# The last expert's rows kept in the second half, and the two halves added to the residual apart

## The chip, the core and the metric

The program runs on one core of a Trainium2 chip. The metric is the device time of one execution in microseconds; it covers two trunk layers for 128 context tokens and 256 latent tokens, that is three tiles of 128 tokens.

## What is computed

```python
def trunk_layer(x, cond, p, mixer, rope, ctx):
    sh1, sc1, g1, sh2, sc2, g2 = adaln(cond, p['w_ada'], p['b_ada'])
    h = rms_norm(x, p['g_norm1']) * (1 + sc1) + sh1
    y, state = mixer(h, p, rope, ctx)
    x = x + g1 * y
    h = rms_norm(x, p['g_norm2']) * (1 + sc2) + sh2
    x = x + g2 * hier_moe(h, p)          # the change is here
    return x, state

def hier_moe(h, p):                      # 4 groups of 8 experts, best group, best 2 experts in it
    ...
    wk, ik = lax.top_k(pe, TOP_K)
    wk = wk / jnp.sum(wk, -1, keepdims=True)
    ...
    hh = jax.nn.silu(h1) * h3 * gate[:, :, None].astype(t.dtype)
    return jnp.einsum('tef,efd->td', hh, p['w2']).reshape(bn, n, d)
```

Layer 0's mixer is a gated MLP beside windowed attention, layer 1's is latent attention: projections of the normed tiles to 672 latent columns, their expansion to heads, attention. All is float32. Each token goes through two of 32 experts; the product with a gate may be done after the expert.

## The kernel before

All orders are written out by hand. Each engine has its own program, and they wait for one another's semaphores. SyncE issues nearly all loads in a fixed order: an order that waits holds up all loads behind it. GpSimd issues the gathers and the stores of expert rows.

**Experts.** Experts are taken in 32 steps; step e computes expert e // 2 + e % 2 * 16, so the last step is that of expert 31. Each has 64 token places; what doesn't fit goes to overflow blocks. Per step: TensorE multiplies 64 tokens by w1 and w3 (L943, 32 records), ScalarE and VectorE form silu(h1) * h3 (L1604, L2350), TensorE transposes it (L949) and multiplies by w2 (L956), ScalarE copies the result to one of two buffers (L1618), and GpSimd stores it row by row to `expert_rows` in HBM (L2826). This tensor has two halves of 384 rows: a token's first pick is written to row t of the first half and its second pick to the same row of the second half. `row_numbers`, worked out in VectorE's `router` for all tokens and experts, says which. "Expert 30's store" below is that of step 30, "expert 29's" that of step 29. The semaphores `y_out0` and `y_out1` count the stores of even and of odd steps.

**The end of a layer.** SyncE's `rows_stored` (L627) waits until all stores of both buffers have landed. `load_pair` (L633) then loads, for tile t, 128 rows of each half, 512 KB each. `load_state` (L621) loads the residual, which was put into HBM in the meantime, back to `x_tiles`. ScalarE's `scale_pair` (L1669) multiplies the first half by its gate. VectorE's `combine` does three operations of 128 x 1024: adds the gated second half (L2459), multiplies by G, which holds the modulation row g2 (L2462), and adds to the residual (L2464).

**What follows in layer 0.** Layer 1 starts in the same place. TensorE: transposes and two expansions of the cached latents (`transpose_c`, `expand`, L1308), products that nobody reads (`keep_running(8, 2)`, L790), and then per tile the transposes of the normed tile (`transpose_h`, L766) and the projection (`project1`, L1258). Tile 1's transposes stand after twelve of tile 0's sixteen products, tile 2's after twelve of tile 1's. VectorE: evacuation of the latents, `unit(0)` (L2628 to L2641: sums over heads, scales of the keys, with a square root on ScalarE between), `combine(0, 0)`, norm of tile 0 (L1976, L1978, after ScalarE's sum of squares L1508), evacuation with modulation (L2038), `combine(0, 1)`, norm, `unit(1)`, evacuation, `combine(0, 2)`, and so on. ScalarE has its own list with `unit`, `scale_pair`, `rms` and its half of the evacuations.

**At the end of layer 1** nothing follows but the three tiles' `combine` and the stores of the output, which ScalarE issues tile by tile.

## Time and profile before

| | |
|---|---|
| median of 3 runs | 978.43 us (975.48 to 981.66) |
| profiled execution | 978.13 us, span 976.3 us, mean granted clock 0.976 |
| TensorE busy | 896.2 us (92%) |
| VectorE, ScalarE, GpSimd busy | 409.5, 239.9, 120.2 us |
| DMA | 318.85 MB, mean 327 GB/s |

The time of the profiled execution includes 1.83 us around its span (first to last instruction). Busy shares are means over stages with different limits. In rows of the timeline the first number is the start in us, the second the time from the start of the first instruction to the end of the last of the row; in brackets stands how long the engine had been idle and what ended that.

### The profile page before, as it was taken

To read this page: it belongs to the slowest core of one execution; us is meant where nothing else is said; L and a number is where in the kernel's file an instruction comes from. 1 tells how busy PE (TensorE), PEld (TensorE's weight loads), DVE (VectorE), ACT (ScalarE), POOL (GpSimd) and SP (SyncE) were. 2 spreads that over 40 slices of the span, in tenths; PEclk is the share of its full clock that TensorE was granted. 3 is DMA by queue.
4 is the path that set the end of the run, shared out by engine and by line. 5 is a ranking of instruction groups with operands and counts; after the bars stand their busy time and mean duration, and the time that the engine had idled before them with its cause. 6 is when DMAs were issued, how large, how long until landed. Compare 5 with 4: busy or idle time off the path is not lost.

```text
span 976.3 us, 14476 instructions
## 1 busy us (share of the span) xinstructions
PE 896.2 (92%) x5479; PEld 503.0 (52%) x5479; DVE 409.5 (42%) x1193; ACT 239.9 (25%) x605; POOL 120.2 (12%) x131
## 2 busy tenths in 40 slices
PE   6999989999999999888999988999989999998880
PEld 3346447556555565455366554554655555645540
DVE  2112476346522442211364576662764225222114
ACT  4020243112111111111354455442211111111111
POOL 1000000100222221211100000001002222212110
PEclk9999999999999999999999999998999999999996
DMA  9999799739999999998870039507599999999975
GB/s 373 397 406 417 292 419 419 247 142 370 364 416 418 402 417 416 418 419 328 330 254 7 1 116 351 234 1 237 212 419 415 417 418 409 417 417 418 412 297 202
DMA packets 62133, 318.85 MB, mean 327 GB/s; under 512 B 12662, under 2 KB 14198, under 8 KB 32104
## 3 DMA queue, kind: packets, MB, share of 16 engines
q1 hardware_dynamic: 46864, 287.51, 72.7%
q0 software_dynamic: 13328, 25.02, 7.4%
q10 hardware_dynamic: 1872, 5.39, 1.5%
q8 instruction: 45, 0.74, 0.3%
q14 instruction: 24, 0.20, 0.1%
HBM read 312.72 MB, written 26.49 MB: 347 GB/s over the span
## 4 chain that ended last, share of the span: by engine, by line
PE 66%; DMA 19%; DVE 9%; issue 2%; ACT 2%; SPq 1%; ACTq 0%; DVEq 0%; POOLq 0%
PE psum L943 15%; DMA ring<-in_l_w 15%; PE psum L956 9%; PE psum L1185 6%; PE psum L1308 3%; PE psum L892 3%; PE psum L879 3%; PE psum L1317 2%; PE psum L923 2%; DMA ring<-in_l_w_ada 2%; PE psum L790 2%; PE psum L1436 2%; PE psum L726 2%; PE psum L1349 2%; PE psum L1411 1%
## 5 line engine op out<-in xcount | busy, mean ns | idle before, releaser
L943 PE MATMUL psum<-ring,scratch 128*64 128x256 f32 x1744 | 210.5, 393 | 22.1 <-DMA ring<-in_l_w 21.1
L943 PEld LDWEIGHTS psum<-ring,scratch 128*64 128x64 f32 x1744 | 135.8, 141 | 81.4 <-issue 32.0
L2350 DVE TENSOR_TENSOR scratch<-scratch,psum 64x256 f32<-64x256 f32 x64 | 27.1, 424 | 286.1 <-ACT scratch L1604 278.9
L956 PE MATMUL psum<-ring,scratch 128*64 128x512 f32 x464 | 112.1, 603 | 1.9 <-ACT scratch L1652 1.0
L2826 POOL DMA_INDIRECT expert_rows<-scratch,slot_rows x64 | 63.5, 992 | 337.5 <-ACT scratch L1618 332.9
L1604 ACT ACTIVATE scratch<-psum 64x256 f32<-64x256 f32 x64 | 24.0, 375 | 255.9 <-PE psum L943 255.9
L1618 ACT COPY scratch<-psum 128x512 f32<-128x512 f32 x64 | 37.5, 585 | 132.1 <-PE psum L956 129.9
L1185 PE MATMUL psum<-ring,scratch 128*128 128x512 f32 (+1 forms) x168 | 63.6, 533 | 0.0
L956 PEld LDWEIGHTS psum<-ring,scratch 128*64 128x64 f32 x464 | 29.3, 136 | 41.5 <-issue 37.3
L1185 PEld LDWEIGHTS psum<-ring,scratch 128*128 128x128 f32 x168 | 31.1, 191 | 29.7 <-issue 28.7
L2332 DVE COPY scratch<-psum 128x512 f32<-128x512 f32 x64 | 41.4, 687 | 7.8 <-PE psum L905 6.9
L949 PEld LDWEIGHTS psum<-constants,scratch 128*128 128x128 f32 x132 | 13.3, 141 | 53.9 <-issue 44.6
L790 PE MATMUL psum<-constants 128*128 128x512 f32 x64 | 31.9, 635 | 7.8 <-DMA constants<-in_shape_constants 7.2
L1826 ACT ACTIVATE scratch<-psum,softmax_stats,latent_stats 128x384 f32<-128x384 f32 (+1 forms) x48 | 28.3, 595 | 41.9 <-DVE softmax_stats L2679 41.9
L2818 POOL DMA_INDIRECT scale_shift<-token_rows_hbm,slot_tokens x30 | 31.2, 1041 | 51.7 <-DVE slot_tokens L2345 44.4
L923 PE MATMUL psum<-constants,scale_shift 128*128 128x128 f32 x240 | 32.8, 280 | 2.2 <-DMA scale_shift<-token_rows_hbm,slot_tokens 2.2
L923 PEld LDWEIGHTS psum<-constants,scale_shift 128*128 128x128 f32 x240 | 25.7, 141 | 13.8 <-issue 10.8
L726 PE MATMUL psum<-ring,scT 128*32 128x512 f32 x256 | 30.2, 597 | 2.0 <-DMA ring<-in_l_w_ada 2.0
L949 PE MATMUL psum<-constants,scratch 128*128 128x128 f32 x132 | 28.9, 301 | 3.1 <-DVE scratch L2350 3.1
L1258 PE MATMUL psum<-ring,scratch 128*128 128x384 f32 (+1 forms) x96 | 28.1, 448 | 1.7 <-ACT scratch L1538 1.6
L1308 PE MATMUL psum<-ring 128*128 128x512 f32 x64 | 28.7, 594 | 0.6 <-issue 0.6
L879 PE MATMUL psum<-ring,scratch 128*128 128x512 f32 x64 | 27.8, 593 | 0.0
(393 smaller groups left out, 1242.3 us busy)
## 6 DMA issues: line engine op xcount, KB each, us to landing
ring<-in_l_w SPq DMA_DIRECT2D x108, 1024.0 KB
ring<-in_l_w_rows SPq DMA_DIRECT2D x56, 1024.0 KB
ring<-in_l_w_ada SPq DMA_DIRECT2D x39, 1024.0 KB, 4.9
ring<-in_ada_first SPq DMA_DIRECT2D x8, 1024.0 KB
ring<-in_l_w_o SPq DMA_DIRECT2D x8, 1024.0 KB
ring<-in_l_w_in SPq DMA_DIRECT2D x4, 1024.0 KB
gate_rows<-gate_rows_hbm POOLq DMA_DIRECT2D x8, 512.0 KB, 7.6
scale_shift<-gate_rows_hbm POOLq DMA_DIRECT2D x8, 512.0 KB, 9.9
```

The lines of the kernel that those rows point to most:

```text
L726: last = nc.tensor.matmul(ps[32 * j:32 * j + 32, ada_bank(l, r), :], scT[:, k, :], ring[:, unit % RING, j * 512:(j + 1) * 512], start=k == ...
L790: nc.tensor.matmul(ps[:, bank, :], ident, over(ident, 1, [P, 4, P]), start=True, stop=True)
L879: last = nc.tensor.matmul(ps[:, base + hf, :], catT_of(n)[:, k, :], ring[:, (U_WO[0] + k // 2) % RING, k % 2 * D + hf * 512:k % 2 * D + (h ...
L923: last = nc.tensor.transpose(ps[:, half, k * P:(k + 1) * P], xg[:, buf, at:at + P], ident)
L943: last = nc.tensor.matmul(ps[64 * n:64 * n + 64, 2 + par, 0:DE], mine[:, k, :], part(w, k * DE, DE), start=k == 0, stop=k == KD - 1)
L949: last = nc.tensor.transpose(ps[:, 4, k * P:(k + 1) * P], hh[:, k * P:(k + 1) * P], ident)
L956: last = nc.tensor.matmul(ps[64 * n:64 * n + 64, 5 + par, :], hhT[:, par, k, :], part(w2, k * D + n * 512, 512), start=k == 0, stop=k == 1)
L1185: last = nc.tensor.matmul(ps[:, 2 * t + n, 0:c1 - c0], hT[:, t, k, :], ring[:, unit % RING, at + c0:at + c1], start=k == 0, stop=k == KD - 1)
L1308: last = nc.tensor.matmul(ps[:, bank + q, :], ckvT[:, t, k, :], ring[:, (U_UKV + k) % RING, at:at + 512], start=k == 0, stop=k == 1)
L1618: nc.scalar.copy(ysb[:, par, :], ps[:, 5 + par, :]).then_inc(S["y_evac"], 1)
L2332: V.tensor_copy(xT[:, buf, part, :], ps[:, half, :].rearrange("p (k s) -> p k s", s=P))\
L2826: pool.indirect_dma_start(Y.rearrange("r (n d) -> (r n) d", n=2), idx, ysb[:, e % 2, :], None, bounds_check=2 * RESULT_ROWS - 1, oob_is_er ...
```

## The change

The rows of the last expert are always written to the second half. For a token whose first pick is expert 31, its two rows are exchanged (`turned` marks such tokens) and its two gates too. With that the first half is complete without the last store. SyncE waits for all stores but that one (`first_rows_stored`), loads the first half of each tile, waits for the last store (`second_rows_stored`) and loads the second half. The first rows lie elsewhere in SBUF (`pair`), where they can be written before the last expert is through. ScalarE's scaling is gone. VectorE adds each half by itself, in two operations: (rows x gate) x G, and the sum to the residual. For the exchange VectorE's routing has one more operation before the rank is taken, two in `route_blocks`, two in `route_overflow`, eight in `route_gates`. Expert 31 isn't a candidate for the one expert that gets two sets of places. In layer 0 the order of loads changes (states of tiles 1 and 2 earlier, the latent weights before the second half of tile 2), VectorE adds the first halves of tiles 0 and 1 ahead of `unit(0)`, and `keep_running(8, 2)` becomes `keep_running(3, 2)`. Left out of the diff are the names of semaphores and SyncE's list at the end of layer 1, which is as told.

```diff
@@ -175,6 +177,7 @@
     c[:, C_CAND:C_CAND + NE] = np.where(np.arange(NE) % PAIRS * 2 >= FIXED, NE - np.arange(NE), 0)
+    c[:, C_CAND + LAST] = 0
     c[:, C_HOME + HOME] = 0.5
@@ -332,7 +335,9 @@
         def pair(t, k):
-            return view(W, 6144 + (2 * t + k) * D, D) if t < 2 else view(AB, (2 + k) * D, D)
+            if k == 0:
+                return view(W, t * D, D)
+            return view(W, 7168 + 2 * t * D, D) if t < 2 else view(AB, 3 * D, D)
         slotm = view(W, 6400, NT, NB)
@@ -620,17 +625,23 @@
                 sp.dma_start(x[:, t, :], X[l][t * P:(t + 1) * P, :]).then_inc(S[f"x{t}_in"], 16)
-            def rows_stored(l):
+            def first_rows_stored(l):
                 sp.wait_ge(S[f"ov_out{l}"], 16)
-                for buf in range(2):
-                    sp.wait_ge(S[f"y_out{buf}"], 16 * (l + 1) * PAIRS)
-            def load_pair(l, t):
-                for k in range(2):
-                    landed = S[f"second_rows{t}" if k and t < 2 else f"pair_rows{t}"]
-                    sp.dma_start(pair(t, k), Y[(k * NT + t) * P:(k * NT + t + 1) * P, :]).then_inc(landed, 16)
+                sp.wait_ge(S["y_out0"], 16 * (l + 1) * PAIRS)
+                sp.wait_ge(S["y_out1"], 16 * (l + 1) * PAIRS - 16)
+            def load_first_rows(l, t):
+                sp.dma_start(pair(t, 0), Y[t * P:(t + 1) * P, :]).then_inc(S[f"first_rows{t}"], 16)
+            def second_rows_stored(l):
+                sp.wait_ge(S["y_out1"], 16 * (l + 1) * PAIRS)
+            def load_second_rows(l, t):
+                sp.dma_start(pair(t, 1), Y[(NT + t) * P:(NT + t + 1) * P, :]).then_inc(S[f"second_rows{t}"], 16)
             def load_first_state(t):
@@ -670,17 +681,20 @@
             load_state(0, 0)
-            rows_stored(0)
-            load_pair(0, 0)
-            load_state(0, 1)
-            load_pair(0, 1)
+            first_rows_stored(0)
+            load_first_rows(0, 0)
+            for t in range(1, NT):
+                load_state(0, t)
+                load_first_rows(0, t)
+            second_rows_stored(0)
+            load_second_rows(0, 0)
+            load_second_rows(0, 1)
             for n, (k0, k1) in enumerate(((0, 3), (3, 6), (6, 8))):
...
                      A["l1_w_in"][k0 * P:k1 * P, :].rearrange("(k p) n -> p k n", p=P), k1 - k0)
-            load_state(0, 2)
-            load_pair(0, 2)
-            sp.wait_ge(S["pair_rows2"], 32)
+            load_second_rows(0, 2)
+            sp.wait_ge(S["second_rows2"], 16)
             for k in range(3):
@@ -1443,7 +1460,7 @@
             expand(1)
-            keep_running(8, 2)
+            keep_running(3, 2)
             transpose_h(2, h3, 0)
@@ -1663,11 +1680,6 @@
                 act.end_ifs()
-            def scale_pair(l, t):
-                act.wait_ge(S[f"pair_rows{t}"], (16 if t < 2 else 32) * (l + 1))
-                nc.scalar.activation(pair(t, 0), pair(t, 0), ACT.Identity, scale=gates[:, t, 0:1]).then_inc(S["pair_scaled"], 1)
             def router(l):
@@ -1839,13 +1851,10 @@
             unit(0)
-            scale_pair(0, 0)
-            scale_pair(0, 1)
             rms(2, (0,))
...
             unit(1)
-            scale_pair(0, 2)
             evac_h(2, hT, 1)
@@ -2214,8 +2223,10 @@
                 V.tensor_tensor(e21, top[2], top[1], ALU.subtract).then_inc(S["eexp_in"], 1)
+                link(V.scalar_tensor_tensor(out=turned_base, in0=pick2[0][:, :, LAST], scalar=-float(RESULT_ROWS),
+                                            in1=con[:, C_ROWHI:C_ROWHI + NT], op0=ALU.mult, op1=ALU.add))
                 link(V.scalar_tensor_tensor(out=row_numbers, in0=pick2[1], scalar=float(RESULT_ROWS),
-                                            in1=over(con[:, C_ROWHI:C_ROWHI + NT], 2, [P, NT, NE]), op0=ALU.mult, op1=ALU.add))
+                                            in1=over(turned_base, 2, [P, NT, NE]), op0=ALU.mult, op1=ALU.add))
                 dve.wait_ge(S["rank_in_psum"], l + 1)
@@ -2230,6 +2241,8 @@
             def route_blocks(l):
+                V.tensor_scalar(row_numbers[:, :, LAST], con[:, C_ROWHI:C_ROWHI + NT], float(RESULT_ROWS), None, ALU.add)
+                V.tensor_copy(turned, pick2[0][:, :, LAST])
                 V.tensor_scalar(nover, cnt, float(SLOTS), None, ALU.is_gt)
@@ -2296,7 +2309,9 @@
                     if k:
-                        link(V.scalar_tensor_tensor(out=ov_row_numbers, in0=hit, scalar=float(RESULT_ROWS),
+                        link(V.tensor_tensor(ov_row_numbers, hit, over(turned, 2, [P, NT, OVER + 1]), ALU.subtract))
+                        link(V.tensor_tensor(ov_row_numbers, ov_row_numbers, ov_row_numbers, ALU.mult))
+                        link(V.scalar_tensor_tensor(out=ov_row_numbers, in0=ov_row_numbers, scalar=float(RESULT_ROWS),
                                                     in1=over(con[:, C_ROW:C_ROW + NT], 2, [P, NT, OVER + 1]),
@@ -2320,6 +2335,13 @@
                 link(V.tensor_tensor(wk[:, :, 1], e21, wk[:, :, 0], ALU.mult))
+                moved, kept = blks, mods
+                for k in range(2):
+                    link(V.tensor_tensor(moved[:, k, :], wk[:, :, k], turned, ALU.mult))
+                    link(V.tensor_tensor(kept[:, k, :], wk[:, :, k], moved[:, k, :], ALU.subtract))
+                for k in range(2):
+                    last = V.tensor_tensor(wk[:, :, k], kept[:, k, :], moved[:, 1 - k, :], ALU.add)
+                link(last)
                 link(V.tensor_tensor(gates[:, :, :], wk, over(pg, 2, [P, NT, 2]), ALU.mult))
@@ -2448,20 +2470,21 @@
                 dve.sem_inc(S["ov_passed"], 1)
-            def combine(l, t):
-                if t < 2:
-                    dve.wait_ge(S[f"second_rows{t}"], 16 * (l + 1))
-                else:
-                    dve.wait_ge(S["pair_rows2"], 32 * (l + 1))
-                p0, p1 = pair(t, 0), pair(t, 1)
-                dve.wait_ge(S["pair_scaled"], 3 * l + t + 1)
-                link(V.scalar_tensor_tensor(out=p0, in0=p1, scalar=gates[:, t, 1:2], in1=p0,
-                                            op0=ALU.mult, op1=ALU.add))
+            def add_first_rows(l, t):
                 dve.wait_ge(S["g2_in"], 32 * (l + 1))
-                link(V.tensor_tensor(p0, p0, G[:, cond_of(t), :], ALU.mult))
+                dve.wait_ge(S[f"first_rows{t}"], 16 * (l + 1))
+                link(V.scalar_tensor_tensor(out=pair(t, 0), in0=pair(t, 0), scalar=gates[:, t, 0:1], in1=G[:, cond_of(t), :],
+                                            op0=ALU.mult, op1=ALU.mult))
                 dve.wait_ge(S[f"x{t}_in"], 16 * (l + 2))
-                V.tensor_tensor(x[:, t, :], x[:, t, :], p0, ALU.add).then_inc(S["x_updated"], 1)
+                link(V.tensor_tensor(x[:, t, :], x[:, t, :], pair(t, 0), ALU.add))
+            def add_second_rows(l, t):
+                dve.wait_ge(S[f"second_rows{t}"], 16 * (l + 1))
+                link(V.scalar_tensor_tensor(out=pair(t, 1), in0=pair(t, 1), scalar=gates[:, t, 1:2], in1=G[:, cond_of(t), :],
+                                            op0=ALU.mult, op1=ALU.mult))
+                V.tensor_tensor(x[:, t, :], x[:, t, :], pair(t, 1), ALU.add).then_inc(S["x_updated"], 1)
                 dve.wait_ge(S["x_updated"], 6 * l + 4 + t)
@@ -2728,15 +2751,18 @@
             link(V.tensor_tensor(kr[:, 3, :], ckvw[:, 3, KV_LORA:], gkr, ALU.mult))
+            add_first_rows(0, 0)
+            add_first_rows(0, 1)
             unit(0)
-            combine(0, 0)
+            add_second_rows(0, 0)
             norm(2, 0)
             evac_h(2, hT, 0)
-            combine(0, 1)
+            add_second_rows(0, 1)
             norm(2, 1)
...
             evac_h(2, hT, 1)
-            combine(0, 2)
+            add_first_rows(0, 2)
+            add_second_rows(0, 2)
             read_c(0)
@@ -2789,7 +2815,9 @@
             for t in range(NT):
-                combine(1, t)
+                add_first_rows(1, t)
+            for t in range(NT):
+                add_second_rows(1, t)
         @block.gpsimd
```

VectorE at layer 0's handover before, from the cached key's gain (L2730) to the norm of tile 0 (L1976, L1978); L2628 to L2641 is unit(0), L2459 to L2464 combine(0, 0):

```order
L2730 TENSOR_TENSOR ring<-ring,params 128x32
L2628 TENSOR_REDUCE latent_stats<-scale_shift 128x8
L2629 TENSOR_SCALAR latent_stats<-latent_stats 128x8
L2637 RECIPROCAL latent_stats<-latent_stats 128x8
L2638 TENSOR_SCALAR latent_stats<-latent_stats 128x8
L2639 TENSOR_TENSOR ring<-psum,latent_stats 128x8x64
L2641 TENSOR_TENSOR ring<-ring,latent_stats 128x8x32
L2459 SCALAR_TENSOR_TENSOR scratch<-scratch,gates 128x1024
L2462 TENSOR_TENSOR scratch<-scratch,gate_rows 128x1024
L2464 TENSOR_TENSOR x_tiles<-x_tiles,scratch 128x1024
L1976 RECIPROCAL sums_of_squares<-sums_of_squares 128x1
L1978 TENSOR_SCALAR scratch<-x_tiles,sums_of_squares 128x1024
```

VectorE now, right behind the cached key's gain; L2477 and L2480 add first rows, L2485 and L2487 second rows, L2651 to L2664 is unit(0):

```order
L2477 SCALAR_TENSOR_TENSOR scratch<-scratch,gates,gate_rows 128x1024
L2480 TENSOR_TENSOR x_tiles<-x_tiles,scratch 128x1024
L2477 SCALAR_TENSOR_TENSOR scratch<-scratch,gates,gate_rows 128x1024
L2480 TENSOR_TENSOR x_tiles<-x_tiles,scratch 128x1024
L2651 TENSOR_REDUCE latent_stats<-scale_shift 128x8
L2652 TENSOR_SCALAR latent_stats<-latent_stats 128x8
L2660 RECIPROCAL latent_stats<-latent_stats 128x8
L2661 TENSOR_SCALAR latent_stats<-latent_stats 128x8
L2662 TENSOR_TENSOR ring<-psum,latent_stats 128x8x64
L2664 TENSOR_TENSOR ring<-ring,latent_stats 128x8x32
L2485 SCALAR_TENSOR_TENSOR scratch<-scratch,gates,gate_rows 128x1024
L2487 TENSOR_TENSOR x_tiles<-x_tiles,scratch 128x1024
```

Four large operations stand ahead of unit(0), and two follow it before the norm, where three stood.

SyncE at the same place before (L633 loads rows, L621 a tile's state, L465 the latent weights):

```order
L465 DMA ring<-in_l_w_ukv 128x2048
L621 DMA x_tiles<-token_state_hbm 128x1024
L633 DMA scratch<-expert_rows 128x1024 x2
L621 DMA x_tiles<-token_state_hbm 128x1024
L633 DMA scratch<-expert_rows 128x1024 x2
L465 DMA ring<-in_l_w_in 128x3x672 x2
L465 DMA ring<-in_l_w_in 128x2x672
L621 DMA x_tiles<-token_state_hbm 128x1024
L633 DMA scale_shift<-expert_rows 128x1024 x2
```

SyncE now (L636 first rows, L644 second rows, L626 state, L470 weights):

```order
L470 DMA ring<-in_l_w_ukv 128x2048
L626 DMA x_tiles<-token_state_hbm 128x1024
L636 DMA scratch<-expert_rows 128x1024
L626 DMA x_tiles<-token_state_hbm 128x1024
L636 DMA scratch<-expert_rows 128x1024
L626 DMA x_tiles<-token_state_hbm 128x1024
L636 DMA scratch<-expert_rows 128x1024
L644 DMA scratch<-expert_rows 128x1024 x2
L470 DMA ring<-in_l_w_in 128x3x672 x2
L470 DMA ring<-in_l_w_in 128x2x672
L644 DMA scale_shift<-expert_rows 128x1024
```

All states and first rows are asked for ahead of any second rows; the wait for the last store is ahead of L644.

## Rows read from the trace of the kernel before

**Rows 1.** The page, chain of waits, share of the span by engine:
```profile
PE 66%; DMA 19%; DVE 9%; issue 2%; ACT 2%; SPq 1%; ACTq 0%; DVEq 0%; POOLq 0%
```

**Rows 2.** Timeline, layer 0's handover (start, us busy, engine, line, idle before):
```profile
466.95 1.02 POOL L2826 DMA_INDIRECT expert_rows<-scratch,slot_rows  x1 [5.91 <-ACT scratch L1618]
...
469.89 0.97 POOL L2826 DMA_INDIRECT expert_rows<-scratch,slot_rows  x1 [1.92 <-ACT scratch L1618]
...
473.38 0.80 SPq L633 DMA_DIRECT2D scratch<-expert_rows  x2
...
477.27 0.69 DVE L2628 TENSOR_REDUCE latent_stats<-scale_shift 128x8 f32<-128x512 f32 x1 [4.47 <-ACT scale_shift L1788]
...
479.75 7.03 PE L790 MATMUL psum<-constants 128*128 128x512 f32 x16
...
479.77 0.42 DVE L2641 TENSOR_TENSOR ring<-ring,latent_stats 128x256 f32<-128x256 f32 x1
...
480.10 1.28 DVE L2459 SCALAR_TENSOR_TENSOR scratch<-scratch,gates 128x1024 f32<-128x1024 f32 x1
...
482.68 1.23 DVE L2464 TENSOR_TENSOR x_tiles<-x_tiles,scratch 128x1024 f32<-128x1024 f32 x1
...
486.61 1.04 PE L766 MATMUL psum<-constants,scratch 128*128 128x128 f32 x8
```

**Rows 3.** Instructions on expert_rows: stores of experts 29 (layer 0), 31 (layer 1); one load:
```profile
L2826 POOL DMA_INDIRECT expert_rows<-scratch,slot_rows x1: 1035/1035/1035, 460.0 to 460.0; - x1
...
DMA to landing us min/median/max: 8.4/8.4/8.4
...
L2826 POOL DMA_INDIRECT expert_rows<-scratch,slot_rows x1: 973/973/973, 954.5 to 954.5; - x1
...
DMA to landing us min/median/max: 2.6/2.6/2.6
...
L633 SPq DMA_DIRECT2D scratch<-expert_rows x1: 319/319/319, 957.2 to 957.2; - x1
...
DMA to landing us min/median/max: 3.2/3.2/3.2
```

**Rows 4.** Timeline, tiles 1 and 2 in layer 0's handover:
```profile
496.13 1.04 PE L766 MATMUL psum<-constants,scratch 128*128 128x128 f32 x8
...
498.06 1.36 DVE L2038 TENSOR_SCALAR scratch<-psum,modulation_columns 128x128 f32<-128x128 f32 x4
...
501.91 1.23 DVE L2464 TENSOR_TENSOR x_tiles<-x_tiles,scale_shift 128x1024 f32<-128x1024 f32 x1
...
507.22 1.06 PE L766 MATMUL psum<-constants,scratch 128*128 128x128 f32 x8 [0.68 <-DVE scratch L1978]
```

**Rows 5.** Windows (busy us and count of each engine, PEclk, DMA share, GB/s):
```profile
889.00:893.00 4.00, 3.95 (x22) 2.90 (x24) 0.00 (x0) 0.00 (x0) 0.00 (x0) 0.57 1.02 420
```

**Rows 6.** Timeline, one expert's first 32 products, at each clock level:
```profile
889.05 5.36 PE L943 MATMUL psum<-ring,scratch 128*64 128x256 f32 x32 [3.04 <-DMA ring<-in_l_w]
...
944.90 3.67 PE L943 MATMUL psum<-ring,scratch 128*64 128x256 f32 x32 [0.95 <-DMA ring<-in_l_w]
```

**Rows 7.** Timeline, the end of the program:
```profile
951.70 1.02 POOL L2826 DMA_INDIRECT expert_rows<-scratch,slot_rows  x1 [5.64 <-ACT scratch L1618]
...
960.41 1.15 ACT L1669 ACTIVATE scratch<-scratch,gates 128x1024 f32<-128x1024 f32 x1 [6.71 <-DMA scratch<-expert_rows]
...
961.72 1.28 DVE L2459 SCALAR_TENSOR_TENSOR scratch<-scratch,gates 128x1024 f32<-128x1024 f32 x1 [12.27 <-DMA scratch<-expert_rows]
...
971.97 1.22 DVE L2464 TENSOR_TENSOR x_tiles<-x_tiles,scale_shift 128x1024 f32<-128x1024 f32 x1
```

**Rows 8.** Timeline, layer 1: rank; expert 16's product and the transposes using it:
```profile
712.90 0.26 DVE L2222 SCALAR_TENSOR_TENSOR scratch<-psum,scratch 128x96 f32<-128x96 f32 x1 [1.00 <-PE psum L1114]
...
828.53 0.42 DVE L2350 TENSOR_TENSOR scratch<-scratch,psum 64x256 f32<-64x256 f32 x1
...
830.11 0.44 PE L949 MATMUL psum<-constants,scratch 128*128 128x128 f32 x2
```

More of the change, by code:

```diff
@@ L1884, in _ @@
             experts(1)
-            for t in range(NT):
-                scale_pair(1, t)
             for t in range(NT):
@@ L2791, in _ @@
             for t in range(NT):
-                combine(1, t)
+                add_first_rows(1, t)
+            for t in range(NT):
+                add_second_rows(1, t)
         @block.gpsimd
```

12 lines of the change are left out of this document (8 added, 4 removed).

## The prediction

> **What bounds the kernel now.** I read the page first: its chain of waits gives TensorE 66% and DMA 19% of the span [rows 1], so in most places a VectorE operation more or less costs nothing. The change works at two others, where a layer's expert results are fetched back and added to the residual. There I read the timeline, because only it shows who is late.
>
> After layer 0's experts, TensorE multiplies latents until 479.75, then runs eight filler products for 7.03 us, and the transposes of the normed tile 0 start at 486.61 [rows 2]. They need VectorE: three operations on tile 0 end at 482.68 + 1.23 = 483.91, ScalarE's sum of squares and the norm follow, 2.6 us in all. VectorE was not held up by rows there: the row L2459 at 480.10 shows no idle time before it, it follows L2641 of unit(0). Later it is VectorE again: the transposes of tile 2 at 507.22 waited for the norm (L1978), which waited for the three operations that end at 501.91 + 1.23 = 503.14 [rows 4].
>
> At the end nothing but VectorE stands on the path: nine operations from 961.72 to 971.97 + 1.22 = 973.19 [rows 7], that is 11.47 / 9 = 1.274 us each, and then the last store. Its first operation waited 12.27 us for rows.
>
> **What the change does to each.**
>
> *Operations.* Before, a tile costs ScalarE one scaling and VectorE three operations. Now VectorE does all of it, in four: scale by gate and by G, add, for each half. ScalarE loses work that was never late. VectorE gets 3 x 1.274 = 3.8 us more per layer. The split pays only if two of the four run while VectorE would have idled.
>
> *The end of the program.* First rows wait for all stores but expert 31's. Expert 30's is issued at 951.70 [rows 7]. A store into quiet queues landed 2.6 us after its issue, a load of rows 3.2 us after [rows 3]. So first rows of tile 0 are there at 951.70 + 2.6 + 3.2 = 957.5, 4.2 us before the 961.72 of now. From there VectorE has twelve operations, 12 x 1.274 = 15.3, end 972.8: **-0.4 us**. The second rows hide: VectorE asks for them at 957.5 + 7.6 = 965.1. Expert 31's store is issued 2.8 us after 30's and, if the first rows' loads slow it to the 8.4 us of a store in a full stream [rows 3], its rows come at 954.5 + 8.4 + 3.2 = 966.1, 1.0 us late. Bounds -0.4 and +1.3; I take -0.4, since the queue is nearly empty there.
>
> *The handover in layer 0.* Order on VectorE is now: first rows of tiles 0 and 1, unit(0), second rows of tile 0. unit(0) cannot end before some 480.1 whatever comes first, as its sums wait for TensorE and ScalarE until 477.27 [rows 2]. So only what VectorE can do before 477.3 is free. When do first rows come? Expert 30's store is issued at 466.95. From below, 2.6 us as at the end: 469.6. From above, SyncE's row at 473.38: by then both stores had landed, so 6.4 us at most. Expert 31's took under 3.5 (469.89 to 473.38) in a stream that was running dry, expert 29's 8.4 in a full one [rows 2, 3]. I take the middle of 3.4 and 6.4: 466.95 + 4.9 = 471.9. Then
> - first rows of tile 0: 471.9 + 3.2 = 475.1. Two operations, 2.55: 477.7.
> - tile 1's rows stand in the queue behind its state, two transfers of 1.3 us (the 1.3 is the step between the uses of the first and second loaded rows, 960.41 and 961.72 [rows 7]): 477.7. Two operations: 480.3.
> - unit(0), which now runs from 477.27 to 479.77 + 0.42 = 480.19, 2.9 us with its own wait for ScalarE: 483.2.
> - second rows of tile 0 (landed near 481.6, five transfers behind the first) two operations: 485.7.
>
> That is 1.8 us **later** than 483.91. VectorE used to do 3 large operations before tile 0 could go on and now does 6, and its free time before 477.3 holds only one pair. With the norm as now, the transposes come at 486.6 + 1.8 = 488.4. From there TensorE's twelve projection products (no change) lead to tile 1's transposes 1.8 later. VectorE's evacuation of tile 1, at 498.06, was set by unit(1), 0.9 us behind TensorE's transposes (496.13 + 1.04) [rows 4]; tile 1 has one operation less there, so that slack goes: +1.0 at the end of this evacuation. Then tile 2 has all four operations in a row, 5.1 us instead of the 3.7 from 499.42 (498.06 + 1.36) to 503.14: +1.3. Tile 2's transposes come **+2.3 us** late. What follows in layer 1 is TensorE nearly without a gap, and the weight stream of layer 1's experts starts when that is through, so I carry it in full to the end.
>
> *Filler products.* Eight are now three: 7.03 x 3/8 = 2.6 us, over at 482.4. TensorE then idles until 488.4, 6.0 us. In the trace it stood 3.04 us for a DMA before 889.05 [rows 6], and the granted clock was 0.57 from 889 to 893 [rows 5]: the lower level (1.2 GHz) for most of it. The 32 products there took 5.36 us against 3.67 at the full level (2.4 GHz) [rows 6]: 1.7 us lost by one fall. Here the idle stretch is twice as long, and what comes after it is on the path: **+1.7 us**. Bounds: 0 if it doesn't fall, 3.4 for two such pieces, since TensorE waits again right after the transposes, for the evacuation. Had the tile been ready at 482.4, cutting fillers would have been worth up to 4.2 us; unit(0) alone excludes that. The Trainium skill (TensorE: Matmul & The Clock Gate, What's actually happening) says that throttled is the default and activity releases it; by that rule the fillers removed have to be paid for, and the rows above agree. If it did not hold here, the sum would be lower by the 1.7.
>
> *Routing.* One operation before the rank: VectorE idles 1.00 us for the rank there. Two in route_overflow (0.2 us each): expert 16's product at 828.53 would be 0.4 us later, ends at 829.4, and TensorE takes it at 830.11 [rows 8]. Two in route_blocks and eight of three columns in route_gates stand beside expert products. All hidden: 0; at most 0.4 a layer if one isn't. Excluding expert 31 from the candidates for the doubled place changes nothing for these inputs: counted from the reference's routing, the only experts with over 64 tokens are number 30 in layer 0 and number 5 in layer 1.
>
> *SyncE.* States and first rows of all tiles go before the second rows, the latent weights after second rows of tile 1, and second rows of tile 2 last. It is the same number of bytes; the latent weights are asked for by TensorE at 490 and come some 8 us after the second rows' issue at 474 to 475. Hidden.
>
> **The sum.** The profiled execution took 978.13 (span 976.30 and 1.83 around it), 0.3 below the median of three, 978.43. 978.13 + 2.3 + 1.7 - 0.4 = **981.7 us**.
>
> **Rivals.**
> 1. *First rows early (faster).* Mechanism: the store of expert 30 takes 2.6 us in layer 0 too. First rows at 472.8; pairs end at 475.4 and 478.0; unit(0) 480.9; tile 0 483.4, 0.5 earlier than now. Tile 1's evacuation then gains 1.4 (the slack and the operation less), tile 2 gives 1.3 back; without a fall of the clock, -0.2 - 0.4: **977.5**. It decides at a landing before about 470.5. For it: the 2.6 us of rows 3. Against: the second half of w_ukv and tile 0's state are issued just ahead of the store. The Trainium skill (DMA: Bandwidth & Descriptors, Anatomy of one DMA) gives about 2.0 us and bytes over 436 GB/s, an estimate of 2.6 for 256 KB: the row at the end agrees, the 8.4 doesn't, as the rule knows no queue. Chance 0.18.
> 2. *Clock holds.* As forecast without the 1.7: **980.0**. For it: one fall in the rows is thin ground. Against: the wait is twice as long as the one before that fall. Chance 0.16.
> 3. *Clock low for two pieces, stores late.* Stores land at 473.4 (+1.5), clock +3.4, second rows late at the end (+1.4): **986**. Chance 0.13.
> 4. *The change doesn't do what it says:* first rows land no earlier than now, because 30's store completes only with 31's. Then layer 0 is +3.8 with the clock +1.7, and the end 960.4 + 15.3 = 975.7, +2.5: **986**. Against: the stores are 2.8 us apart in both layers. Chance 0.06.
> 5. My forecast, **981.7**, chance 0.47.
>
> **How the numbers follow.** A measurement of this kernel tells about 1% from no change (975.48 to 981.66 are three runs of one kernel). 1% is 9.8 us: faster by that needs what no case gives (0.02); slower, 988.2, lies 2 us above rivals 3 and 4 (0.05). Within 1%: 0.93. The range leaves out the tops of rivals 3 and 4 and the bottom of rival 1: 976.0 to 986.5.
>
> **What would show it.** In the new trace: the load of first rows issued at 470 to 473 in layer 0; pairs of large VectorE operations before unit(0)'s reduction, which moves from 477.3 to about 480; TensorE idle for some 6 us before tile 0's transposes and granted clock 0.5 near 485 to 492; tile 2's transposes 4 us after their place now; at the end twelve large operations without a gap from about 957.5 + 4. I am wrong if tile 0's transposes start before 486.6, if the clock stays at 1.0, or if VectorE waits between first and second rows at the end.

## The result: 989 us, slower by 1.1%

| | median us | executions | range us | ratio to before, 95% interval |
|---|---|---|---|---|
| before | 977.81 | 4 | 975.48 to 981.66 | |
| changed | 989.09 | 4 | 985.21 to 990.23 | 1.0107 (1.0076 to 1.0139) |
| changed, measured again with the experiments | 987.02 | 4 | 983.67 to 990.60 | 1.0095 (1.0057 to 1.0132) |

The execution with a trace took 990.23 us (span 988.4), the slowest of its four, and is set against the traced one of before, 978.13.

The chain of waits on the page of the changed kernel, which stands against [rows 1]: TensorE's share has grown by 3 points of a longer span, VectorE's has not.

```profile
PE 69%; DMA 18%; DVE 9%; ACT 2%; issue 2%; SPq 1%; ACTq 0%; DVEq 0%; POOLq 0%
```

The place is found on the timeline of layer 0's handover, against [rows 2]:

```profile
466.24 1.02 POOL L2854 DMA_INDIRECT expert_rows<-scratch,slot_rows  x1 [5.99 <-ACT scratch L1635]
...
472.78 0.33 SPq L636 DMA_DIRECT2D scratch<-expert_rows  x1
...
476.17 1.29 DVE L2477 SCALAR_TENSOR_TENSOR scratch<-scratch,gates,gate_rows 128x1024 f32<-128x1024 f32 x1 [4.08 <-DMA scratch<-expert_rows]
...
479.03 2.74 PE L807 MATMUL psum<-constants 128*128 128x512 f32 x6
480.06 1.28 DVE L2477 SCALAR_TENSOR_TENSOR scratch<-scratch,gates,gate_rows 128x1024 f32<-128x1024 f32 x1 [1.34 <-DMA scratch<-expert_rows]
...
482.63 0.69 DVE L2651 TENSOR_REDUCE latent_stats<-scale_shift 128x8 f32<-128x512 f32 x1
...
486.77 1.23 DVE L2487 TENSOR_TENSOR x_tiles<-x_tiles,scratch 128x1024 f32<-128x1024 f32 x1
...
490.62 1.97 PE L783 MATMUL psum<-constants,scratch 128*128 128x128 f32 x8 [8.85 <-DVE scratch L1985]
494.18 9.13 PE L1275 MATMUL psum<-ring,scratch 128*128 128x384 f32 x24 [1.60 <-ACT scratch L1555]
...
503.15 1.04 PE L783 MATMUL psum<-constants,scratch 128*128 128x128 f32 x8
...
504.23 1.37 DVE L2045 TENSOR_SCALAR scratch<-psum,modulation_columns 128x128 f32<-128x128 f32 x4 [2.40 <-PE psum L783]
...
514.71 1.06 PE L783 MATMUL psum<-constants,scratch 128*128 128x128 f32 x8 [1.48 <-DVE scratch L1985]
```

The clock that TensorE was granted there (the column behind POOL's; 0.50 is 1.2 GHz, 1.00 is 2.4), in windows of 4 us:

```profile
487.00:491.00 4.00, 0.38 (x2) 0.39 (x3) 1.92 (x3) 1.44 (x3) 0.00 (x0) 0.50 1.04 417
...
495.00:499.00 4.00, 4.00 (x10) 2.48 (x9) 2.32 (x5) 2.49 (x5) 0.00 (x0) 0.57 1.01 413
499.00:503.00 4.00, 4.00 (x16) 2.71 (x15) 2.35 (x7) 0.32 (x2) 0.00 (x0) 1.00 0.95 377
```

Read it from the left. The fillers start at 479.03, 0.7 us earlier than before, so the layer before it cost nothing. The residual of tile 0 ends at 486.77 + 1.23 = 488.00, 8.97 us after that start, where it was 4.16 (483.91 and 479.75): **4.8 us later**. The transposes run at half clock (1.97 us where 1.04 stood) and the 24 products behind them take 9.13 us; at full clock they took 7.05 in the trace of before. That is 3.0 us more. Tile 2's transposes come at 514.71, **7.5 us** after their place in [rows 4], 8.2 after the same start.

The rest is in layer 1. Its first rows and products, in the changed kernel and then in the one before:

```profile
713.40 7.09 PE L807 MATMUL psum<-constants 128*128 128x512 f32 x12
...
721.41 0.26 DVE L2233 SCALAR_TENSOR_TENSOR scratch<-psum,scratch 128x96 f32<-128x96 f32 x1 [1.75 <-PE psum L1131]
...
739.87 1.16 PE L940 MATMUL psum<-constants,scale_shift 128*128 128x128 f32 x8 [2.99 <-DMA scale_shift<-token_rows_hbm,slot_tokens]
740.96 3.52 PE L973 MATMUL psum<-ring,scratch 128*64 128x512 f32 x8
...
744.52 0.80 SPq L506 DMA_DIRECT2D ring<-in_l_w  x2
...
956.06 5.21 PE L960 MATMUL psum<-ring,scratch 128*64 128x256 f32 x32 [2.14 <-DMA ring<-in_l_w]
```

```profile
705.83 5.40 PE L790 MATMUL psum<-constants 128*128 128x512 f32 x12
...
730.56 1.09 PE L923 MATMUL psum<-constants,scale_shift 128*128 128x128 f32 x8 [2.20 <-DMA scale_shift<-token_rows_hbm,slot_tokens]
731.58 1.94 PE L956 MATMUL psum<-ring,scratch 128*64 128x512 f32 x8
...
733.56 0.81 SPq L501 DMA_DIRECT2D ring<-in_l_w  x2
```

The delay is 7.6 us at the router's fillers, 8.5 when VectorE takes the rank (721.41; 712.90 in [rows 8]), 9.4 at the first expert's down projection (L973; L956 before), and 11.0 when SyncE asks for the next weights. The first and the last of these steps are pieces at half clock: fillers of 7.09 us for 5.40, of which 0.9 reaches the rank, and the down projection, 3.52 for 1.94. The step between is 0.8 us more of waiting for the first gathered rows (2.99 for 2.20). The last expert (956.06; [rows 6] has 3.67 us for the same products at full clock) adds 1.5. The last stores are 12.7 us late.

At the end, against [rows 7]:

```profile
964.40 1.02 POOL L2854 DMA_INDIRECT expert_rows<-scratch,slot_rows  x1 [8.38 <-ACT scratch L1635]
...
966.62 1.27 SPq L636 DMA_DIRECT2D scratch<-expert_rows  x3
967.17 0.97 POOL L2854 DMA_INDIRECT expert_rows<-scratch,slot_rows  x1 [1.76 <-ACT scratch L1635]
969.85 1.28 DVE L2477 SCALAR_TENSOR_TENSOR scratch<-scratch,gates,gate_rows 128x1024 f32<-128x1024 f32 x1 [7.71 <-DMA scratch<-expert_rows]
...
973.78 0.80 SPq L644 DMA_DIRECT2D scratch<-expert_rows  x2
...
984.07 1.23 DVE L2487 TENSOR_TENSOR x_tiles<-x_tiles,scale_shift 128x1024 f32<-128x1024 f32 x1
```

Twelve operations without a gap, from 969.85 to 985.30. From the issue of expert 30's store to the end of the last operation it is 20.9 us; it was 21.5 (951.70 to 973.19). So the end **gives back 0.6 us** here. Over all traces of the experiments below and these two, the same stretch is 20.9 to 21.6 us in the ten with the changed end and 21.5 to 21.7 in the six with the old one. The sum of the trace: 8.2 - 0.7 in the handover, 5.2 in layer 1, -0.6 at the end, 12.1.

### The profile page after: what moved, and what is told of

It reads as the page before. It is cut to its first block, busy times and chain, and to the rows that moved or that the text cites. A ratio compares the mean times of both kernels' runs of the same rounds, so it can differ in the third digit from the quotient of the medians.

```text
span 988.4 us, 14476 instructions
## 1 busy us (share of the span) xinstructions
PE 895.1 (91%) x5469; PEld 501.8 (51%) x5469; DVE 420.4 (43%) x1221; ACT 233.4 (24%) x599; POOL 120.8 (12%) x131
## 4 chain that ended last, share of the span: by engine, by line
PE 69%; DMA 18%; DVE 9%; ACT 2%; issue 2%; SPq 1%; ACTq 0%; DVEq 0%; POOLq 0%
PE psum L960 17%; DMA ring<-in_l_w 14%; PE psum L973 9%; PE psum L1202 6%; PE psum L909 3%; PE psum L896 3%; PE psum L1334 2%; PE psum L940 2%; PE psum L1325 2%; PE psum L1275 2%; PE psum L807 2%; PE psum L1453 2%; PE psum L743 2%; PE psum L1366 2%; PE psum L1428 1%
## 5 line engine op out<-in xcount | busy, mean ns | idle before, releaser
L960 PE MATMUL psum<-ring,scratch 128*64 128x256 f32 x1744 | 207.0, 388 | 27.5 <-DMA ring<-in_l_w 26.6
L973 PE MATMUL psum<-ring,scratch 128*64 128x512 f32 x464 | 113.7, 610 | 1.9 <-ACT scratch L1669 1.0
L973 PEld LDWEIGHTS psum<-ring,scratch 128*64 128x64 f32 x464 | 29.6, 137 | 42.1 <-issue 38.0
## 6 DMA issues: line engine op xcount, KB each, us to landing
ring<-in_l_w_in SPq DMA_DIRECT2D x4, 1024.0 KB, 21.5
```

Source lines behind the costliest of these rows:

```text
L960: last = nc.tensor.matmul(ps[64 * n:64 * n + 64, 2 + par, 0:DE], mine[:, k, :], part(w, k * DE, DE), start=k == 0, stop=k == KD - 1)
L973: last = nc.tensor.matmul(ps[64 * n:64 * n + 64, 5 + par, :], hhT[:, par, k, :], part(w2, k * D + n * 512, 512), start=k == 0, stop=k == 1)
```

## The experiments

"Shift" below is the start of tile 2's transposes after the start of the fillers, less the 27.47 us (479.75 to 507.22) of before, from the one trace of each kernel. Medians are of 4 to 10 executions. Those of before are of 14 to 28 on the same chip (977.28 to 977.93), and of 4 for the first row (977.81). The ratio with its interval is worked out by itself and can differ a little from the quotient of the two medians: for 16 fillers that quotient is 1.0063.

| kernel | shift | median | ratio, 95% interval |
|---|---|---|---|
| changed | +8.2 | 989.09 | 1.0107 (1.0076 to 1.0139) |
| changed, again | +5.7 | 987.02 | 1.0095 (1.0057 to 1.0132) |
| changed, 8 fillers | +6.1 | 986.88 | 1.0098 (1.0074 to 1.0123) |
| changed, 14 fillers | +5.6 | 987.21 | 1.0090 (1.0058 to 1.0121) |
| changed, end as before | +5.3 | 986.03 | 1.0089 (1.0058 to 1.0119) |
| 8 fillers, 5 more in layer 1 | +7.7 | 988.47 | 1.0094 (1.0062 to 1.0126) |
| 8 fillers, tile 1's first rows later | +6.5 | 983.55 | 1.0064 (1.0041 to 1.0088) |
| only tile 0's rows apart, 8 fillers | +3.8 | 978.92 | 1.0017 (0.9991 to 1.0042) |
| the same, 12 fillers | +3.4 | 980.51 | 1.0027 (1.0009 to 1.0046) |
| layer 0 as before, end changed | 0 | 976.99 | 0.9997 (0.9972 to 1.0022) |
| the same, 5 fillers in layer 1 | 0 | 977.05 | 0.9993 (0.9977 to 1.0010) |
| only the router's part | 0 | 977.44 | 1.0009 (0.9987 to 1.0031) |
| before, 3 fillers | +2.9 | 981.42 | 1.0041 (1.0015 to 1.0066) |
| before, 16 fillers | +6.9 | 983.60 | 1.0047 (1.0028 to 1.0065) |
| before, 24 fillers, 6 operations | +13.7 | 992.85 | 1.0148 (1.0117 to 1.0179) |

**Which part costs.** Three kernels with parts of the change put back. First the end alone (cut down; the old places of the rows and the semaphores are left out):

```
-            first_rows_stored(0); load_first_rows(0, 0) ...
+            first_rows_stored(0); second_rows_stored(0)
+            load_pair(0, 0); load_state(0, 1); load_pair(0, 1) ...
-            add_first_rows(0, 0); add_first_rows(0, 1); unit(0); add_second_rows(0, 0) ...
+            unit(0); combine(0, 0) ...        # ScalarE scales, 8 fillers
```

> The changed kernel with layer 0's handover as before (loads in pairs, ScalarE scales the first rows, three large VectorE operations to a tile, eight fillers); the end of layer 1 and the router stay as changed. Theory A (all of the loss is made in layer 0's handover): at or below the kernel before; the end of the program gives 0.4 to 0.6 us, so 977 to 978. Theory C (the router's added operations cost in layer 1): the later +4 us of the trace stay: 981 to 982. If the changed end itself is slower: above 979 with the experts' stores at the same time as before.

976.99 us, 0.9997: with layer 0's handover as it was, nothing of the loss is left. Then the same with layer 1's end put back too, so that only the routing differs from before:

> The kernel before with nothing but the router's part of the change: the last expert's rows always in the second half, and the small VectorE operations for it. Both handovers as before. Theory A: within 0.5 us of before, 978. Theory C: +1 us in each layer at the router and +2 to +3 through the weight stream in layer 1: 981 to 982.

977.44, 1.0009: no cost of the added small operations shows. This interval alone would leave room for 3 us; that of the kernel above, which has them too, ends at 1.0022. And the end alone put back:

```
-            first_rows_stored(1); load_first_rows(1, t) ... second_rows_stored(1); load_second_rows(1, t)
+            first_rows_stored(1); second_rows_stored(1); load_pair(1, t)
-            add_first_rows(1, t) ... add_second_rows(1, t)
+            combine(1, t)                     # ScalarE scales
```

> The changed kernel with the end of layer 1 as before (all stores, then pairs; ScalarE scales; nine large operations). Layer 0's handover and the router as changed. Theory A: all of the loss stays and the small gain at the end goes: 989 to 990. If the end's new order is what costs: well below the changed kernel, 980 or less.

986.03, 1.0089: 3 us below the forecast, but the loss is still there. So it is made by what the change does in layer 0's handover. The small gain at the end is below what this comparison can tell; the traces show it (above).

**The fillers.** `keep_running(3, 2)` to `keep_running(8, 2)` in the changed kernel:

> The changed kernel with one number put back: eight filler products on TensorE ahead of tile 0's transposes in layer 0's handover, where the change left three. The order on VectorE stays as changed. Theory A (VectorE's order): tile 0's transposes still wait for the residual on VectorE, which ends at 488.00 in the changed kernel's trace, so only the clock after it can improve: the transposes 1.97 us back to 1.04, and the first products after them 9 us back to 7. About 2 to 4 us of the 11.3 come back: 985 to 987. Theory B (the fillers are the cause: TensorE idles 8.85 us and falls to half clock): the time comes back but for about 2 us, near 980. Theory C (the router's added small operations): nothing changes, 989.

986.88, 1.0098: theory A, at its upper edge. In the trace the fillers ended at 484.80, the transposes came 3.07 us later, and the clock had fallen all the same:

```profile
487.87 1.97 PE L783 MATMUL psum<-constants,scratch 128*128 128x128 f32 x8 [3.07 <-DVE scratch L1985]
491.43 8.52 PE L1275 MATMUL psum<-ring,scratch 128*128 128x384 f32 x24 [1.59 <-ACT scratch L1555]
```

So five more fillers did not prevent the fall, they only shortened the idle stretch. With 14:

> The changed kernel with 14 filler products where it has 3 (with 8 the products ended 3.1 us ahead of tile 0's transposes, and these ran at half clock all the same). 14 last 6.2 us where 3 lasted 1.3 to 2.7, and end near or a little before the transposes. Theory: the clock holds, the transposes take 1.04 us, the products behind them 7.05; against eight fillers 2 to 2.5 us less, near 984.5. Rival, that the fillers don't matter beyond eight: 986.9.

```profile
482.50 12.18 PE L807 MATMUL psum<-constants 128*128 128x512 f32 x28
...
494.52 1.04 PE L783 MATMUL psum<-constants,scratch 128*128 128x128 f32 x8
```

The clock held, as expected, but the median is 987.21 and not 984.5: the fillers themselves now stand in the way. Tile 0 was normed at 491.96 (L1985, 491.20 + 0.76), TensorE was free at 494.5. What the clock gave, the fillers took. The converse, three fillers in the kernel before:

> The kernel before with three filler products where it has eight, nothing else. VectorE still sets tile 0's transposes at 486.6, so TensorE now idles 4.2 us ahead of them in place of nothing. If idle time is what lowers the clock here, the transposes take 1.97 us in place of 1.04 and the products behind them some 1.5 to 2 us more, as in the changed kernel's trace: +2.5 to +3, near 980. If the clock holds over 4.2 us: 977.3, no change.

```profile
486.48 1.97 PE L766 MATMUL psum<-constants,scratch 128*128 128x128 f32 x8 [4.03 <-DVE scratch L1978]
...
490.04 10.00 PE L1258 MATMUL psum<-ring,scratch 128*128 128x384 f32 x24 [1.59 <-ACT scratch L1538]
```

981.42, 1.0041: a fall of the clock at this place costs (1.97 - 1.04) + (10.00 - 7.05) = 3.9 us of TensorE's time here, and 3.5 us in the median. The same number costs 3.5 us in one kernel and nothing that can be told in the other (986.88 with eight, 989.09 and 987.02 with three), since in the changed one the clock falls with three and with eight.

**The order on VectorE.**

```
             add_first_rows(0, 0)
-            add_first_rows(0, 1)
             unit(0)
             add_second_rows(0, 0); norm(2, 0); evac_h(2, hT, 0)
+            add_first_rows(0, 1)
             add_second_rows(0, 1)
```

> The changed kernel with eight fillers, and on VectorE the first rows of tile 1 added after tile 0's columns are evacuated, next to its second rows, where the change adds them ahead of unit(0). All loads and all twelve large operations as changed. Theory (two large operations and the wait for tile 1's rows ahead of unit(0) are what delays the handover): tile 0's residual ends about 2.5 us earlier than with eight fillers alone, tile 2's transposes 3 to 4 us earlier; the four operations of tiles 1 and 2 stay, +1.3 each at most. 979 to 982, against 986.9. Rival (reading all rows apart costs whatever the order): 986.

983.55, 1.0064: 3.3 us less than with eight fillers alone, less than forecast. The reason stands in its trace. With tile 1 out of the way, VectorE waits for tile 0's second rows, which were hidden until then:

```profile
483.74 1.28 DVE L2485 SCALAR_TENSOR_TENSOR scratch<-scratch,gates,gate_rows 128x1024 f32<-128x1024 f32 x1 [2.37 <-DMA scratch<-expert_rows]
```

They had been asked for at 474.87, 8.9 us before, behind the first rows of three tiles and the states of two. So the order of SyncE's queue costs too. The handover in this trace is therefore hardly earlier: counted from the fillers' start, tile 0's residual ends 0.3 us sooner than with eight fillers alone and tile 2's transposes come 0.4 us later, where I had expected 2.5 and 3 to 4 us sooner. The trace doesn't show where the median gained its 3.3 us, and the two intervals (up to 1.0088, from 1.0074) overlap. Both are undone in the next kernel, which reads only tile 0 apart and leaves tiles 1 and 2 as before, the place of the latent weights in SyncE's list too. Only the new lines are shown:

```
+            load_first_rows(0, 0); second_rows_stored(0); load_second_rows(0, 0)
+            load_state(0, 1); load_pair(0, 1) ...
+            add_first_rows(0, 0); unit(0); add_second_rows(0, 0); norm(2, 0); evac_h(2, hT, 0)
+            combine(0, 1) ... combine(0, 2)      # three operations, ScalarE scales
```

> The changed kernel where in layer 0 only tile 0's rows are read and added apart: first rows of tile 0 as soon as they are stored, before unit(0); its second rows after unit(0); tiles 1 and 2 as before (in pairs, scaled on ScalarE, three VectorE operations). Eight fillers. The end of layer 1 as changed. Theory: VectorE's free time ahead of unit(0) holds one pair of large operations and no more, so it is the two operations of tile 1 ahead of unit(0), and tile 2's fourth, that cost. Tile 0's residual then ends within 1 us of its place before, and the time is within 1 us of the kernel before: 976.5 to 978. Rival, that reading rows apart is late in itself (more DMAs ahead of the second rows, the stores' landing): 980 or more.

978.92, 1.0017: another 4.6 us back, 1 us above the range that I gave. In this execution the first rows came only at 478.29, 11.2 us after the issue of expert 30's store (467.06), TensorE idled 1.97 us and its clock fell once more:

```profile
472.86 0.33 SPq L639 DMA_DIRECT2D scratch<-expert_rows  x1
473.63 0.32 SPq L647 DMA_DIRECT2D scratch<-expert_rows  x1
...
478.29 1.28 DVE L2505 SCALAR_TENSOR_TENSOR scratch<-scratch,gates,gate_rows 128x1024 f32<-128x1024 f32 x1 [5.38 <-DMA scratch<-expert_rows]
...
488.85 1.61 PE L791 MATMUL psum<-constants,scratch 128*128 128x128 f32 x8 [1.97 <-DVE scratch L2000]
```

So this kernel shows that the loss goes when both orders are as before; it doesn't part the one from the other. The first two rows matter beyond it: the second rows were asked for 0.8 us after the first, with nothing between them but the wait for expert 31's store. Issued 3.7 us apart (467.06 and 470.75), the two stores had landed at most 0.8 us apart. The profile's own landing times say the same of all nine traces with an early load of first rows: expert 31's store, issued 2.8 to 3.7 us behind expert 30's, landed 0.1 to 0.8 us after that load was asked for. That is all the head start that the split had in layer 0. Twelve fillers for this kernel:

> The kernel in which only tile 0's rows are read apart in layer 0 (978.9), with 12 fillers in place of 8, so that TensorE has no idle time before tile 0's transposes. Theory: the clock no longer falls there (it took 2.6 us in that kernel's trace), and tile 0's residual is the only thing late: 977 to 978. Rival: in executions where the rows come early the four fillers stand in the way of the transposes, up to 1.7 us: no better than 979.

980.51, 1.0027: the rival. The rows came earlier this time (474.21, 9.4 us after the store of 464.80), tile 0's residual ended 0.4 us later than before counted from the fillers' start, and the fillers held the transposes up: 10.3 us of them where 8 take 6.9. How many fillers are right depends on when the rows are there, and that was 8.7 to 11.2 us after the store's issue in the nine traces.

**Is a delay of the handover carried to the end?** Six operations `V.tensor_tensor(p0, p0, p0, ALU.max)` ahead of tile 0's residual, and `keep_running(24, 2)`:

> The kernel before, with tile 0's residual in layer 0's handover delayed by six more large VectorE operations (the maximum of a tile with itself, 6 x 1.23 = 7.4 us), and 24 filler products in place of 8, so that TensorE stays busy over the delay. Router, ends and loads as before. If a late handover is carried to the end in full and no more: +7.4, 984.7. If layer 1 adds to any delay of the handover (the weight stream of its experts, a wait that grows): +10 to +12, 988. If layer 1 takes some of it up: 980 to 983.

992.85, 1.0148. The 24 fillers lasted 20.76 us, longer than the residual was delayed, so the delay was 13.7 us and not 7.4; the median rose by 15.0. A delay near that of the changed kernels, from `keep_running(16, 2)` alone:

> The kernel before with 16 filler products where it has 8, nothing else: they last 14.1 us, so tile 0's transposes start 7.1 us later with TensorE busy all the way. Tile 2's transposes are then where they are in the changed kernels (5.3 to 8.2 us late in their traces), and nothing else is changed. If the 3 us that the changed kernels lose beyond that come from the later place alone (clock falls or waits of layer 1 that a shift brings about): +10, 987 to 988. If they come from something in the changed handover that the traces of one execution each don't show: +7.1, 985 or a little under.

983.60, 1.0047: +6.2 us in the median for a shift of 6.9. By the medians a late handover is carried to the end about one to one (by the ratio, 4.6 for the 6.9), and layer 1 adds at most some 1 us to it by itself.

**What layer 1 adds in the changed kernels.** Two kernels with five fillers where TensorE waits for the first gathered rows (`if l and e == 1: keep_running(5, 5)` ahead of that wait):

> The kernel with layer 0's handover as before and the end as changed (977.0), and five filler products on TensorE in layer 1 after expert 1's up projection, where it waits 2.0 to 3.0 us for the gathered rows. Theory (the clock falls in that wait in most executions: the first expert's down projection took 3.1 to 3.7 us in seven of ten traces against 1.94 in the others, and that holds the weight stream up): the down projection takes 1.94 us, the experts' stretch is 2 to 3 us shorter than with the fall, median 975 to 976. Rival (the weight stream makes up for the fall, or the fillers only delay the transposes): 977.

> The changed kernel with eight fillers (986.9) and the same five filler products in layer 1's wait for the gathered rows. It asks where the some 3 us come from that the changed kernels lose beyond the 6 to 8 us of the handover. Theory (falls of the clock in that wait, more often there): 983 to 984. Rival (they are lost elsewhere): within 1 us of 986.9.

The down projection took 1.94 us in both, so the fall was gone, and the median did not move: 977.05 after 976.99, and 988.47 after 986.88. With the end alone changed, from TensorE's first gather (L929) to the issue of expert 30's store it was 240.1 us with the fillers and 241.2 without (709.38 to 949.45, 709.86 to 951.01). The trace with eight fillers alone had no fall at that place to begin with (1.94 us). This fall isn't what the changed kernels lose, and it is worth less than a measurement can tell. The changed kernel once more, for a second trace:

> The changed kernel as it is, for a second trace: which of its delays are there in every execution. Theory: tile 2's transposes start 47 to 49 us after the issue of expert 30's store (48.5 in the first trace, 40.3 before), and the first rows are there 9 to 10 us after that issue; the clock falls in layer 1 change their places. 989, give or take 1.5. Rival: the first trace was a late one, with 986 or less and 44 to 46 us here.

987.02, 1.0095, and a shift of 5.7: 46.0 us from expert 30's store (467.32) to tile 2's transposes (513.32). The stretch is at the rival's upper edge, the median between rival and theory. The first trace was a late one by 2.5 us in the handover, though the loss is there in both.

## Why the prediction was wrong

I said 981.7, within 976.0 to 986.5, and gave 0.05 to slower by over 1%. The result is 989.1, 2.6 above the range. The step that failed is the handover in layer 0 and the sentence that carries it "in full to the end". My sum added 3.6 us to the traced execution, and the trace has 12.1. Of the 8.5 between them, 4.2 are in the handover (8.2 by the fillers' start for my 4.0: tile 0's residual +4.8 for +1.8, the clock 3.0 for 1.7) and 5.2 in layer 1, which I had put at nothing; the fillers' earlier start takes back 0.7, the end 0.2.

*Right.* That the end gives 0.4: it gave 0.6 in the first trace, and over all traces the median of that stretch is 21.2 us against 21.6. Expert 30's store landed in 2.2 us and its rows in 3.2, where I had 2.6 and 3.2; the twelve operations ran without a gap; expert 31's store landed in 6.6 (967.17 to 973.78) and its rows were hidden, though just: in three of the ten traces with the changed end VectorE waited 0.20 to 0.47 us for them. (My upper bound of +1.3 there doesn't come out of its own working: rows 1.0 us late turn -0.4 into +0.6.) Routing at nothing: 1.0009, and 0.9997 together with the changed end. That VectorE before unit(0) sets the handover, that TensorE idles and its clock falls, that tile 1's evacuation gives back some 0.8 (504.23 is 6.2 after its place, the transposes 7.0), and that tile 2 then pays 1.3 (7.5 after 6.2). That a delay is carried in full is so where fillers alone make it (+6.2 for 6.9); in the changed kernels layer 1 added to it.

*First rows at 475.1.* This failed, by the store's landing. I took 4.9 us, the middle of 3.4 and 6.4. It was 6.5 in the first trace (466.24 to 472.78), 5.1 in the second (467.32 to 472.39), and 5.1 to 6.5 in the nine traces of kernels that don't wait for expert 31's. The seven that wait for that as well took 5.6 to 7.1 from the same issue: hardly more. In layer 0 both stores landed within about 1 us of each other in every trace that tells it (472.78 and 472.87 in the first), though issued 2.8 to 3.7 us apart, and the lower part of my interval, down to 3.4, was never seen.

*Tile 1's rows at 477.7, one transfer pair behind.* They came at 480.06 in the first trace and VectorE stood 1.34 us for them (0.23 in the second, not at all with eight fillers), with unit(0) and tile 0's second rows queued behind that wait. I had named what is queued behind the operations, and let the rows come in time.

*Tile 0's residual +1.8.* By the same start it was +4.8, +3.3 with eight fillers, +2.6 in the second trace of the changed kernel (480.11 to 486.85). The mechanism was as I put it, the size too small by 0.8 to 3.0.

*Clock +1.7.* Mis-sized: 3.0 in the first trace, 3.9 in the kernel before with three fillers, 2.4 to 4.0 in all traces where it fell there. I had priced one fall by one group of 32 products. Here more work lies in it: the transposes (+0.9) and, after 1.6 us without work, the products behind them (+2.1 in the first trace, 1.4 to 3.0 in all). My upper bound of 3.4, for two such pieces, was nearer, and two traces are above it.

*The fillers as the cause of the fall.* Wrong in the changed kernel, as 8 fillers show. They would have to cover VectorE's delay as well, and then they delay by themselves.

*What is still open.* By the traces the changed handovers cost 5.3 to 8.2 us, the medians of the kernels that have tile 1's first rows ahead of unit(0) (the first six rows of the table) lie 8 to 11 us above before. Some 3 us are not accounted for. They aren't the routing (0.9997 with it and the changed end), not the end (1.0089 with it as before), and not the later place, which costs 6.2 by the median and 4.6 by the ratio for a shift of 6.9. They seem to go with the order of tile 1's first rows: put later, with all loads as they were, the excess is gone (shift 6.5, median 5.6 above), though four executions of one kernel don't show that beyond doubt. The traces give one hint. In windows of 5 us from 650 to 760, the time times what the clock lacks adds up to 6.8 us in three of the six traces of these kernels (the changed one twice, and with eight fillers) and to 1.7 to 3.5 in the others; in the other kernels it is 0 to 3.4, and 5.1 in one, the kernel before with three fillers. Layer 1's own length goes with it. From tile 2's transposes to expert 30's store it is 444.5 us before (507.22 to 951.70), 449.7, 448.5 and 447.8 in the three traces with 6.8, and 448.5 in the one with 5.1; of the nine with 1.7 or less, eight have 442.9 to 445.4 and one 446.8. So in the traces most of what layer 1 adds is time at half clock, and it is not peculiar to the changed order. What in a handover brings such falls about some 170 us later, and whether they are the missing 3 us of the medians, was not tried.

Of the rivals, number 3 (stores late, clock low for two pieces, 986) named both terms of the handover that were too small; I gave it 0.13. Number 4 (expert 30's store completes only with 31's) had a chance of 0.06, and in layer 0 its condition nearly held: the two landed within about 1 us. At the end it didn't (966.62 and 973.78). Number 1 needed a landing before 470.5; the earliest that any trace shows is 5.1 us after the store's issue.

## What to carry to other kernels

Splitting a wait in two helps only where the first half is ready clearly earlier and the engine that takes it has idle time and nothing urgent behind it. At the end of this program both held and the split gave 0.4 to 0.6 us by the traces; in the handover the halves were ready at most 0.8 us apart and urgent work stood behind them (unit(0), tile 0's second half, its norm), and the split as made there cost 9 to 10. Put the first half of one tile early at most, its own second half next, and no wait for a later tile ahead of work for an earlier one. Even that gained nothing here: 978.92 us, against 976.99 with the handover left alone. Count filler products together with the delay that they should bridge: too few don't hold the clock, and the ones that do hold it may stand in the way.

## What was not expected of the hardware

The clock is not tied to the length of one idle stretch. It fell after 1.97 us in one kernel above. In layer 1's attention TensorE stands idle 1.81 to 1.82 us before the same six transposes in every trace; in the kernel before they ran partly at half clock after it, and in the kernel with only the end changed, whose code is the same there, at full clock:

```profile
663.71 1.20 PE L1360 MATMUL psum<-constants,scratch 128*128 128x128 f32 x6 [1.81 <-DVE scratch L2689]
664.84 1.55 PE L1376 MATMUL psum<-ring,scale_shift 128*64 128x128 f32 x12
```

```profile
662.64 0.88 PE L1384 MATMUL psum<-constants,scratch 128*128 128x128 f32 x6 [1.81 <-DVE scratch L2740]
663.45 0.88 PE L1400 MATMUL psum<-ring,scale_shift 128*64 128x128 f32 x12
```

The Trainium skill (TensorE: Matmul & The Clock Gate, What's actually happening) says that the monitor behind the gate runs on by itself and doesn't start with the kernel, so that the same code may be slow at a place in one run and not in the next. These rows fit that, though they don't show it to be the reason; they also mean that one trace can't price a fall.

The indirect store of an expert's rows took 2.2 us to land at the end of the program (964.40 to 966.62), 6.6 when the first of three loads of rows was issued half a microsecond ahead of it (966.62; the store 967.17 to 973.78), and 5.1 to 6.5 in layer 0.
